# Four moves in a hybrid attention layer on 8 cores: values projected first, the decay input and the rows of x earlier in each stage, a fourth buffer for rows of x, the last tile's first gates inside the last stage

## What is computed

```python
h = rms_norm(x, g_pre)
proj = h @ w_in                      # qa ka va za qb kb vb zb lr gate_a gate_b, 5648 columns
# mixer A: 4 heads, two softmax maps of head dim 64 each, causal, with ALiBi
p = softmax(qa @ ka.T / 8 - slope * dist)          # for both maps
oa = (p[0] - lam * p[1]) @ va                      # value dim 128
ya = (rms_norm(oa, g_sub_a) * (1 - lam_init) * silu(za)) @ w_up_a
# mixer B: gated linear attention; S_t = diag(alpha_t) S_{t-1} + k_t^T v_t ; o_t = q_t S_t
glog = log_sigmoid(lr @ w_alpha + b_alpha) / 16
yb = (rms_norm(gla(qb, kb, vb, glog), g_sub_b) * silu(zb)) @ w_up_b
y = sigmoid(gate_a) * ya + sigmoid(gate_b) * yb
out = x + rms_norm(y @ w_out, g_post)
```

## Time and profile before

| | |
|---|---|
| runs of the kernel | 1583.32, 1593.0, 1669.48 us; median 1593.0 us |
| profiled execution, its own time | 1584.28 us |
| its span on core 4, first to last instruction | 1582.8 us |
| spans of the eight cores | 1567.3 to 1582.8 us |
| mean granted TensorE clock of the cores | 0.973 to 0.984 |
| busy: TensorE, ScalarE, VectorE, GpSimd | 1414.0, 850.4, 713.1, 473.1 us |

### The profile page before, as it was taken

How to read it: one execution, slowest core, us unless ns; L and a number is a source line. 1 busy time by engine, 2 the same in 40 slices (tenths; PEclk the granted TensorE clock), 3 DMA queues, 4 the chain that set the end, 5 groups by cost and what they waited for, 6 DMA issues and landing times.

```text
span 1582.8 us, 27781 instructions; the slowest of 8 cores (1567.3 to 1582.8 us)
## 1 busy us (share of the span) xinstructions
PE 1414.0 (89%) x10576; PEld 741.1 (47%) x10576; DVE 713.1 (45%) x1453; ACT 850.4 (54%) x1714; POOL 473.1 (30%) x469
## 2 busy tenths in 40 slices
PE   4987798999899978999889998899998999988888
PEld 2443344444454534555445554455554555544443
DVE  3558657633664354623545134453233541233434
ACT  4254355144634554365654665656667557667632
POOL 1035422523343221523225132142221340220441
PEclk9999899999999998999999999999999999999999
DMA  9788687332732344222522224412225322224022
GB/s 267 230 233 257 195 257 245 116 119 88 235 104 94 108 155 152 80 94 94 191 103 80 89 88 138 167 55 89 86 75 179 107 68 68 78 84 161 28 80 106
DMA packets 75437, 207.43 MB, mean 131 GB/s; under 512 B 7984, under 2 KB 26672, under 8 KB 75312
## 3 DMA queue, kind: packets, MB, share of 16 engines
q1 hardware_dynamic: 75312, 205.66, 40.2%
HBM read 173.12 MB, written 32.51 MB: 130 GB/s over the span
## 4 chain that ended last, share of the span: by engine, by line
PE 68%; DVE 13%; ACT 10%; POOL 3%; issue 3%; DMA 2%; SPq 1%; DVEq 0%; POOLq 0%
PE ps_q L270 31%; PE ps_f L270 23%; PE ps_oa L270 13%; ACT sb_PT L996 4%; DVE sb_scr L872 2%; DVE sb_scr L893 2%; ACT sb_junk L890 1%; ACT sb_ztmp L638 1%; DVE sb_wring L383 1%; DVE sb_rz L1022 1%; DVE sb_tmpo L1024 1%; DMA sb_xb<-x 1%; DMA sb_V<-w_in 1%; ACT sb_hT L616 1%; POOL sb_gtA L1050 1%
## 5 line engine op out<-in xcount | busy, mean ns | idle before, releaser
L996 ACT ACTIVATE sb_PT<-ps_q 128x512 bf16<-128x512 f32 (+3 forms) x705 | 370.8, 568 | 215.9 <-PE ps_q L270 125.0
L270 PE MATMUL ps_oa<-sb_V,sb_PT 128*128 128x129 bf16 x4224 | 345.0, 222 | 10.9 <-ACT sb_PT L996 5.2
L270 PEld LDWEIGHTS ps_oa<-sb_V,sb_PT 128*128 128x128 bf16 x4224 | 286.1, 99 | 138.8 <-issue 32.0
L996 ACT ACTIVATE sb_PT<-ps_f 128x512 bf16<-128x512 f32 (+3 forms) x447 | 244.3, 563 | 186.1 <-PE ps_q L270 105.0
L270 PE MATMUL ps_q<-sb_hT,sb_wring 128*128 128x512 bf16 x1016 | 253.9, 385 | 11.9 <-ACT sb_wring L379 3.8
L270 PE MATMUL ps_f<-sb_hT,sb_wring 128*128 128x512 bf16 x776 | 193.9, 382 | 8.0 <-ACT sb_hT L616 3.7
L837 POOL TENSOR_TENSOR sb_yT<-sb_scr 128x512 bf16<-128x512 f32 x64 | 81.6, 1278 | 388.2 <-DVE sb_scr L835 372.0
L270 PE MATMUL ps_q<-sb_QT,sb_KT 64*128 64x512 bf16 (+3 forms) x705 | 161.0, 365 | 17.8 <-DVE sb_yT L639 6.7
L270 PE MATMUL ps_q<-sb_wring,sb_hT 128*128 128x512 bf16 x632 | 163.6, 394 | 8.0 <-DVE sb_szA L639 2.7
L270 PEld LDWEIGHTS ps_q<-sb_hT,sb_wring 128*128 128x128 bf16 x1016 | 91.9, 99 | 123.1 <-issue 41.8
L270 PE MATMUL ps_f<-sb_QT,sb_KT 64*128 64x512 bf16 (+3 forms) x447 | 131.4, 363 | 9.4 <-DVE sb_yT L639 2.1
(11 more groups left out here) (177 smaller groups left out, 1846.3 us busy)
## 6 DMA issues: line engine op xcount, KB each, us to landing
sb_wring<-wsc SPq DMA_DIRECT2D x204, 512.0 KB, 3.8
sb_xb<-x SPq DMA_DIRECT2D x60, 512.0 KB, 5.6
out<-sb_scr SPq DMA_DIRECT2D x32, 512.0 KB, 3.0
wsc<-sb_wring SPq DMA_DIRECT2D x30, 512.0 KB, 9.2
sb_KT<-w_in SPq DMA_DIRECT2D x48, 256.0 KB, 8.2
sb_V<-w_in SPq DMA_DIRECT2D x40, 256.0 KB, 8.2
sb_V<-w_out SPq DMA_DIRECT2D x8, 256.0 KB, 5.9
sb_KT<-w_out SPq DMA_DIRECT2D x8, 256.0 KB, 8.6
```

Source lines behind the costliest of these rows:

```text
L270: P.op("pe", lambda e: e.matmul(out=out_, lhsT=lhsT, rhs=rhs, start=start, stop=stop, **kw), reads=reads, writes=writes)
L996: act(lambda e, pp=pp, m=m, c0=c0, b=b, cbias=cbias: e.activation(out=PT[pp][:, m, c0:512], in_=BANK[b][:, c0:512], func=AF.Exp, bias=cbia ...
```

## The change

1. **Prologue.** The values' weights are loaded first. Each 128 rows of x are normed and transposed, and their values projected at once (`v_row`), for tile 0 and then for tile 1 between chains of q; k comes last. Loads of x are let through in steps (`xlim`), the table `eft` is loaded at the start, and the conversions of waiting pieces may be issued by `tick` only from a set point on (`ahead`), and in the stages already when more than two pieces wait. The up weights can be converted on ScalarE too.
2. **Rows and decay input.** In stages 1 to 7 `u_lr` stands in the middle of the output projection, ahead of its last nine units, and not behind it. `a_units(t+1)` is merged with all but the last four units of `gproj`. `decay2` stands two units later.
3. **Fourth buffer.** From stage 2 on, a piece of V that is not yet used (`XV`) is a fourth buffer for rows of x; its last load comes before tile 7's values need the place.
4. **Last tile's gates.** The two gates with which `u_e(7)` begins are merged into the core of stage 7, whose costs are halved. In the tail each next gate stands ahead of the up projections before it, and two of the four pairs of gates are held in the memory of `hT[0]`.

```diff
+        XV = (V[:, 28:32, :, :].rearrange("p a b c -> p (a b c)")[:, 0:2048].bitcast(F32), ["xv0", "xv1"], "x7")
+        def x_free(i):
+            if i < 7:
+                return XPRO[i]
+            for buf in XBUF + ([XV] if extra[0] and i < len(xseq) - 8 else []):
+                if buf[2] not in x_owner:
+                    return buf
+            return None
...
-        wseq = QKV + SEQ_Z + SEQ_G
+        wseq = QKV[4:6] + QKV[0:4] + SEQ_Z + SEQ_G
...
-        wseq = wseq + SEQ_E0 + SEQ_E
+        wseq = wseq + SEQ_E0 + ["GA1", "GB1", "U0", "GA2", "GB2", "U1", "GA3", "GB3", "U2", "U3"] + [f"WO{i}" for i in range(4)]
...
-            if pend and pend[0][0] <= wst["acq"]:
+            if pend and ahead[0] and (pend[0][0] <= wst["acq"] or len(pend) > 2 and calm[0]):
...
+            last = t + 1 == ntiles
+                own = last and p_ % 2 == 0
+                src = hf if own else scr
...
-            return head, units
+            (h0, u0), (h1, u1), (h2, u2), (h3, u3) = order
+            if last:
+                return h0, h1 + u0 + h2 + u1 + h3 + u2 + u3
+            return h0, u0 + h1 + u1 + h2 + u2 + h3 + u3
...
-            gproj = (u_lr + vbu[0:2] + [w(0.26, alpha(0)), w(0.26, alpha(1))] + vbu[2:4] + [z(soft)] + vbu[4:6] + [z(scan, 0)] + vbu[6:8]
-                     + [z(scan, 1), z(decay, 0)] + zbu[0:2] + [z(decay, 1)] + zbu[2:4] + [z(decay2)] + zbu[4:] + qku)
+            gproj = (vbu[0:2] + [w(0.26, alpha(0)), w(0.26, alpha(1))] + vbu[2:4] + [z(soft)] + vbu[4:6] + [z(scan, 0)] + vbu[6:8]
+                     + [z(scan, 1), z(decay, 0)] + zbu[0:2] + [z(decay, 1)] + zbu[2:6] + [z(decay2)] + zbu[6:] + qku)
             if t >= 1 and t + 1 < ntiles:
-                gproj = merge(gproj, a_units(t + 1))
-            units = units + gproj
+                gproj = merge(gproj[:-4], a_units(t + 1)) + gproj[-4:]
+            if t >= 1:
+                units = units[:-9] + u_lr + units[-9:] + gproj
+            else:
+                units = units + u_lr + gproj
             if t + 1 == ntiles:
-                units = units + core_units(3.0, 1.0, True)
+                units = units + merge(core_units(1.5, 0.5, True), last_e[0])
...
+        def v_row(t, s):
...
+            run_units(chain(8, one, lambda b: ev_v(t, s, b)))
+
         emit_load()
         emit_load()
-        xst["limit"] = 8
-        x_load()
-        run_units(a_units(0))
...
+        xlim(4)
         emit_load()
+        xlim(6)
+        a_stat(0, 0)
+        a_norm(0, 0)
+        take("VA0")
+        a_tr(0, 0)
+        take("VA1")
         emit_load()
+        xlim(8)
...
+        v_row(0, 0)
+        a_stat(0, 1)
+        a_norm(0, 1)
+        a_stat(0, 2)
+        a_tr(0, 1)
+        a_norm(0, 2)
+        v_row(0, 1)
...
-        head, body = u_e(ntiles - 1)
-        tail = head[0:4] + [w(0.4, g_tr, 3)] + head[4:] + body + u_f(ntiles - 1)
+        body = last_e[1]
+        tail = body[0:4] + [w(0.4, g_tr, 3)] + body[4:] + u_f(ntiles - 1)
```

158 lines of the change are left out of this document (101 added, 57 removed).

## The result

| | before | changed |
|---|---|---|
| median of the runs | 1595.3 us (6 runs) | 1569.8 us (6 runs) |
| ratio, 95% interval | | 0.985 (0.980 to 0.990) |
| profiled execution, its span | 1584.3, 1582.8 us | 1569.8, 1568.2 us |
| spans of the eight cores | 1567.3 to 1582.8 us | 1559.3 to 1568.2 us |

A forecast was written before the change was run, and what follows sets the result against it. TensorE, busy 89% of the span, was taken as the bound, with idle time and lower clock to win. Terms 3 + 14 + 7 + 1 + 7 = 32 us, less 5 given back, took 1584.3 to 1557 us; range 1536 to 1580.

The forecast's parts named there:

- the waits only change their names: Rival: five banks and the fins stay, so the middle stages give only 3 us; 1571 us, chance 0.22.
- Prologue: Start of the kernel: loading and projecting values first brings the like point from 73.7 to 71.4 us, taken as 3 us gained.
- all four blocks and both pieces, 4 MB, are there at 17 us: Prologue step: x blocks and value weights land by 17 us, so the fourth values chain ends at about 27 us.
- the early stages would be paced by DMA: Stated way to be wrong: what the prologue wins is waited for again in stage 0 or 1; no chance given.
- Middle stages: Decay input, transposes and fourth buffer together save 22 us, of which 5 us are given back to the next waits.
- The transposes: Ahead of the next tile's q: placing transposes before the last units removes TensorE's waits for their copies; 7 us gained.
- The decay input: End of each output projection: moving it four chains earlier saves 8.5 us of waiting and 5.5 us of clock; 14 us.
- The fourth buffer: Rows of x: ScalarE's 13.0 us of waits shrink, counted as 1 us gained, 0 to 6 us.
- ScalarE stops for x: Rival: earlier squares in stages 1 to 6 stop ScalarE 24 times; at 2 us each, 1592 us, chance 0.05.
- Last gates: Stage 7 and tail: four chains of 1.73 us leave the tail at no cost in stage 7; 7 us gained.
- about 1.4 us of work in them: Stage 7's last steps of 2.95 us hold 1.4 us of TensorE work, so a half gate chain of 0.87 us fits.
- Other edits: decay2's shift, up conversions on ScalarE, early eft and ones_col in three parts, across the stages: together costed at nothing.

The follow-up runs named there:

- E1: The changed kernel with the prologue of the kernel before (q and k first, then values), all else kept; ratio to before 0.977 (0.969 to 0.985).
- E5: The changed kernel with its prologue reordered: rows of x asked for earlier, all four blocks of tile 0 transposed before the first values chain; profiled execution 1563.5 us.
- E11: E5 with tile 0's squares ahead of the first transpose copy and the first q piece converted one chain earlier; ratio to before 0.983, profiled execution 1559.2 us.
- E7: E1 without the fourth buffer, three buffers for rows of x throughout; ratio to before 0.994 (0.992 to 0.996).
- E10: E1 with the decay input back behind the output projection in all stages; ratio to before 0.991 (0.989 to 0.993).
- E4: The kernel before with only the last tile's first two gates moved into stage 7's core and the tail's new gate order; ratio 0.997 (0.995 to 0.998).
- E9: The kernel before with only the fourth buffer and the edits it needs, including the ones in V written in three parts; ratio 1.000 (0.999 to 1.001).
- E6: E1 with decay2 back at its old place, two units earlier; ratio to before 0.988 (0.985 to 0.991).
- E12: E11 with the fourth buffer opened already in stage 1, at the start of the output projection; 1553.3 us, ratio to before 0.979 (0.977 to 0.981).
- E2: The kernel before with only the decay input moved ahead of the output projection's last nine units in stages 1 to 7; ratio 0.999 (0.995 to 1.003).

## Why the prediction was right in its range and off in its terms

The range held the time, and "within 2%" was the likeliest class. The forecast was 12.8 us too low; by the table, where 27 us were forecast (32 less the 5 given back), 13.0 came. So 1569.8 us lie beyond the forecast's own stretch of 1548 to 1568, and 1 us from the 1571 of the rival "the waits only change their names". That nearness is luck: the rival had 3 us from the middle stages and 3 from the prologue, and the runs have 17.7 and a loss of 5.8. Of the signs given for the profile, "wrong if above 77" for the first scores came true (82.5 us), the clock was below 0.98 in stage 1 (0.93), a wait on `gtB` was left in stage 7, the waits on `hT` were 3.6 us and not under 3, and steps of stage 7 took up to 4.7 us and not 3.3; the tail and ScalarE's waits for x were as said.

**Prologue, -3 forecast, +5.8 measured.** This step failed, in its sign. The sentence "all four blocks and both pieces, 4 MB, are there at 17 us" is a sum of bytes. It took no account of the order on SyncE's queue, where rows 1 to 3 stand behind both pieces, nor that the loads of x are let through in steps; and the "5.5 us from the landing of a block to its values" were taken once, not once for each block. The blocks did land about when the sum says (squares at 16.24, 17.65 and 21.10 us), but the second only at 16 us, close to the last. The fourth chain of values ended near 34 us, not 27. The other half is the queueing of squares behind conversions, which I had named and priced at the far end only. E1 shows that all of it is the prologue's, E5 and E11 that its order is at fault and not the idea: mended, values first is 4.1 us faster than the old order, near the -3 of the forecast. That the early stages would be paced by DMA is refuted by E1 and E11: both keep what they win.

**Middle stages, -22 and 5 given back, -17.7 measured.** The sum was right, in part by luck: its parts are not worth what was put down for them, and two of them are worth something only beside others. The transposes give 7.4 us alone, as forecast (7). The decay input gives nothing alone, and 10.6 us beside the rest (14 forecast). The fourth buffer gives nothing alone and 13.1 us beside the rest, stages 0 and 1 included (1 forecast, 0 to 6): this term was mis-sized most. The term of the buffer was sized from the waits of before; but its price is set by the change's own earlier squares. In stage 4, 196.1 us before, each part alone, and two of the three without either the buffer (E7) or the input's move (E10), leave it at 192.0 to 197.2 us, and all three at 184.9. The rows of E7 and E10 point to one place, the fins. With the input in its old place TensorE waits 4.09 us for `gtB`; with the input moved but three buffers, a square comes next, waits 5.12 us for the row whose buffer the fins have just freed, and TensorE waits 4.80. The rival "the waits only change their names" is true for two of the three taken alone, and the changed kernel escapes it. The third pair, input and buffer without the transposes, was not run, so it is not shown that all three are needed. The rival "ScalarE stops for x" is real (E7, and stage 1 of the changed kernel), with stops of 3 to 7 us in stages 1 and 4 and 1 to 4 us elsewhere (21.3 us in 6 stops on core 4 of E7), and not 24 times 2; the fourth buffer prevents it from stage 2 on, as the sentence against it said. The waits that I foresaw at the fins are there in stages 3 (2.74 us, `vb`), 5 (2.7 us, `gaT`) and, shorter, 6 (1.55 us, `gaT`); they went in 1, 2 and 4, but in stage 1 the square took their place.

**Last gates, -7 forecast, -3.9 measured (E4).** The tail went as forecast: 60 us from the last scores to the end of the span, for 61. The failed step is "about 1.4 us of work in them": it counted the scores and half of the products with V.

**Other edits, 0 forecast, +3.8 measured (E9, with its two reserves).** `ones_col(2)` is four casts of VectorE, and I wrote that the first use of their result is far off. That is so, but the cost lies with what stands behind them in the queue: TensorE was waiting for `ps_oa` to be read. decay2's shift was rightly at nothing (E6). In E12 and in all kernels here that stand at 225.8 us or more in stage 7 these 3.8 us are still in; a version with the casts elsewhere was not run, so that they cause it is read from the timeline at 1282.30 us and not shown by a run.

**The clock** is at one of two levels, 1.2 and 2.4 GHz, by the rows (eight chained matmuls in 3.57 or 1.89 us), and a stop of 4 to 5 us costs what it waits and again some 2 to 4 us: E10's eight matmuls take 3.62 us behind it, and stage 4 as a whole has 180.7 us of busy TensorE in E10, 176.9 in the changed kernel (core 1 of both), with the same 1404 matmuls recorded.

**Stage 1.** The input's move costs 2.7 us (E2) and 3.7 us (E10) in stages 0 and 1. There is no fourth buffer there, and the timelines show the exchange: 2.74 us on `gtB` before and in E10, 4.62 us on `vb` in E2, 5.99 in the changed kernel.

The Trainium skill's page "DMA: Bandwidth & Descriptors", section Bandwidth, by which, as an estimate, the prologue would have gained 9 us, gives about 358 GB/s a core when both cores of the HBM domain stream. The trace again does not agree: the changed kernel moved 298 GB/s from 20 to 40 us, at a share of 0.96, and at most 311 in any fortieth of its span.

Open: what makes the waits for `yT` longer (7.2 and 5.4 us before, 12.8 and 5.9 in the changed kernel), whether the waits of E12 for weights would go with another order on SyncE's queue, and what half of the up conversions on ScalarE and the early `eft` are worth, which no run takes by themselves.

## What to carry to other kernels

When several queues meet at one event, taking one wait away can show the next of the same length; price such edits together, and test each by leaving it out as well, since alone two of the three here looked worthless. In a prologue, follow each block through every queue in order (DMA issue, square, scaling, copy): a sum of bytes says when the last comes, not when the second does. The cost of an added instruction is read from what is queued behind it, and not from the user of its result.
